# Prologue and block boundary reordered in a two-block fp32 kernel, and one mask multiply left out of the delta rule

## The reference

```
cond = silu(c); mod = cond @ w_ada + b_ada
sh1, sc1, gt1, sh2, sc2, gt2 = split(mod, 6)
h = rmsnorm(x, g_mix) * (1 + sc1) + sh1
q, k, v, qi, ki, wi, cu = split(h @ w_in)         # rope on q, k, qi, ki by positions
x = x + gt1 * (concat(attention, conformer_conv(cu)) @ w_out)
h = rmsnorm(x, g_mlp) * (1 + sc2) + sh2
x = x + gt2 * (relu(h @ w_up)**2 @ w_down)
x = rmsnorm(x, g_final)                           # end of the first block
u = rmsnorm(x, norm_mix_2); proj = u @ w_in_2     # second block
qkv = silu(causal_conv(proj[P:P+3G])); z, a, b = rest of proj
g = -exp(a_log) * softplus(a + dt_bias); gcum = cumsum(g) in chunks of 64
m = (beta*k @ k^T) * exp(gcum_i - gcum_j) where i > j else 0
attn_inner = (q @ k^T) * exp(gcum_i - gcum_j) where i >= j else 0
(I + m)^-1 applied to [beta*v, beta*k*exp(gcum)]; scan over 16 chunks
x = x + concat(pool, delta_out) @ w_out_2; MLP and norm as above
```

## Time and profile before

| what | value |
|---|---|
| median of three runs | 3015.2 us (3012.55 to 3021.21) |
| the profiled execution | 3020.86 us |
| its span | 3019.0 us |
| busy in the span: TensorE, VectorE, GpSimd, ScalarE | 93%, 58%, 41%, 23% |
| mean granted TensorE clock | 0.962 of full |
| read from HBM | 143.35 MB |

### The profile page before, as it was taken

The page is one execution under the profiler, slowest core; times in us unless marked ns, Lnnn a source line. Parts: engine busy times, 40 slices in busy tenths (PEclk is TensorE's granted clock), DMA queues, the critical chain, the costliest instruction groups (busy, mean ns, idle before and its releaser), DMA issues.

```text
span 3019.0 us, 34563 instructions
## 1 busy us (share of the span) xinstructions
PE 2808.5 (93%) x13488; PEld 2307.2 (76%) x13488; DVE 1758.3 (58%) x2240; ACT 705.0 (23%) x1154; POOL 1248.8 (41%) x815
## 2 busy tenths in 40 slices
PE   4999988899999999999997999688879999999998
PEld 4866867688778888888885767577768888888887
DVE  5257899996556665566566585255534444443335
ACT  5222233343322110000114242222214001110002
POOL 1411277453454443344347323234434443344342
PEclk8979999899999999999998999799999999999999
DMA  6200111110221111111111211000032111111111
GB/s 208 64 8 14 35 43 60 46 55 23 110 72 49 56 50 41 48 56 49 46 49 64 62 35 35 0 1 1 29 111 64 56 49 41 49 56 42 42 56 56
DMA packets 141464, 153.33 MB, mean 51 GB/s; under 512 B 6151, under 2 KB 104228, under 8 KB 141350
## 3 DMA queue, kind: packets, MB, share of 16 engines
q1 hardware_dynamic: 135360, 137.68, 14.6%
q10 hardware_dynamic: 5990, 14.09, 1.3%
HBM read 143.35 MB, written 8.39 MB: 50 GB/s over the span
## 4 chain that ended last, share of the span: by engine, by line
PE 80%; DVE 13%; ACT 3%; issue 2%; POOL 1%; DMA 0%; ACTq 0%; DVEq 0%; POOLq 0%
PE ps L1813 11%; PE ps L1814 11%; PE ps L1815 11%; PE ps L1798 11%; PE ps L1800 10%; PE ps L1799 10%; PE ps L2185 3%; DVE score L1347 3%; DVE best L1345 2%; DVE yt L1628 2%; PE ps L1878 1%; PE ps L1956 1%; PE ps L1879 1%; PE ps L1880 1%; DVE yt L1617 1%
## 5 line engine op out<-in xcount | busy, mean ns | idle before, releaser
L1798 PE MATMUL ps<-h_hi,w_hi 128*128 128x512 f32 x1472 | 592.3, 402 | 17.7 <-issue 11.7
L1800 PE MATMUL ps<-h_hi,w_lo 128*128 128x512 f32 x1472 | 578.9, 393 | 0.0
L1799 PE MATMUL ps<-h_lo,w_hi 128*128 128x512 f32 x1472 | 578.9, 393 | 0.0
L662 POOL TENSOR_TENSOR w_hi<-raw,zero 128x1024 fp32r<-128x1024 f32 x128 | 243.9, 1905 | 780.5 <-PE ps L1800 397.1
L1813 PE MATMUL ps<-w_hi,u_hi 128*128 128x512 f32 x1024 | 399.0, 390 | 0.0
L1814 PE MATMUL ps<-w_lo,u_hi 128*128 128x512 f32 x1024 | 398.8, 389 | 0.0
L1815 PE MATMUL ps<-w_hi,u_lo 128*128 128x512 f32 x1024 | 398.6, 389 | 0.0
L1521 DVE TENSOR_TENSOR act_r<-act_r 128x512 f32<-128x512 f32 x128 | 167.7, 1310 | 328.7 <-ACT act_r L1036 328.7
L1798 PEld LDWEIGHTS ps<-h_hi,w_hi 128*128 128x128 f32 x1472 | 279.7, 190 | 92.6 <-issue 28.7
L665 POOL TENSOR_TENSOR w_lo<-raw,w_hi 128x1024 fp32r<-128x1024 f32 x128 | 337.6, 2638 | 10.0
L1036 ACT ACTIVATE act_r<-ps 128x512 f32<-128x512 f32 x128 | 76.5, 598 | 1130.7 <-PE ps L1800 1130.7
(11 more groups left out here) (380 smaller groups left out, 4503.5 us busy)
## 6 DMA issues: line engine op xcount, KB each, us to landing
raw<-in_w_up_dram SPq DMA_DIRECT2D x64, 512.0 KB, 4.0
raw<-in_w_down_dram SPq DMA_DIRECT2D x64, 512.0 KB, 3.3
raw<-in_w_ada_dram SPq DMA_DIRECT2D x48, 512.0 KB, 3.7
raw<-in_w_in_dram SPq DMA_DIRECT2D x32, 512.0 KB, 3.7
raw<-in_w_out_dram SPq DMA_DIRECT2D x32, 512.0 KB, 3.3
x<-in_x_dram ACTq DMA_DIRECT2D x16, 512.0 KB, 7.6
x_mid<-x SPq DMA_DIRECT2D x8, 512.0 KB, 2.6
x<-x_mid ACTq DMA_DIRECT2D x8, 512.0 KB, 7.4
```

The costliest lines, as they stand in the source:

```text
L662: g_.tensor_tensor(w_hi[:, r, :], raw[:, r, :], zero.to_broadcast([P, 1024]), ALU.add).then_inc(sem("w_hi_done"), 1)
L1798: mm(ps[:, bank, :], wh, h_hi[:, k, cols], start=(k == 0), stop=False)
L1799: mm(ps[:, bank, :], wh, h_lo[:, k, cols], start=False, stop=False)
L1800: last = mm(ps[:, bank, :], wl, h_hi[:, k, cols], start=False, stop=(k == NK - 1))
```

## The change

Prologue: `c` is loaded straight into 128x8 by the first load of ScalarE's queue, and its sigmoid stands after the fifth; the other vectors follow. x is loaded by SP, four tiles after the first four of `w_ada` and four after the sixth. On VectorE the sums come first, without the copies and the angle ahead of them. The tap copies go to ScalarE, the cast of positions to GpSimd, the angle and sines behind `norm0`. `norm0` makes `h_f` alone and VectorE rounds it; its units go by pairs of channels, half 0 and half 1 in turn, and `tm_in(0)` waits for two units at a time. The column sums are made in two parts.

Block boundary: `times_g` goes to VectorE between partial sums 7 and 8; ScalarE writes `h_hi` alone and VectorE takes `h_lo` from PSUM; GpSimd's final scaling is left out, and x is multiplied by `rs` where it is read back (`mixed2`); `ab_half(0)` comes ahead of the turns of half 1, and TensorE goes on with 14 of 16 units.

Delta rule: the steps for g go into the loop, at columns 2, 3, 4 and 18, the first `z` before the last gate product, and the multiply of e1 by `strict` is left out (m is only read through the level masks); `qdec` comes behind `b1`.

```diff
@@ SP @@
+                if n in (4, 6):
+                    for t in range(2 * n - 8, 2 * n - 4):
+                        sp.dma_start(x[:, t, :], a["x"][0, t * P:(t + 1) * P, :]).then_inc(sem(f"x_in{t // 4}"), 16)
...
-                        sp.wait_ge(sem("x_final"), t + 1)
+                        sp.wait_ge(sem("norm_ss"), paired_ss("z", 4 * (t // 4) + 3))
@@ GpSimd @@
+            pool.wait_ge(sem("rows_in"), 16 * (len(VEC) + 3))
+            g.tensor_copy(rowsp, rowsi).then_inc(sem("rowsp_ready"), 1)
...
-            for i in range(3):
-                split2(i)
-            for t in range(4, NT):
-                times_g(t)
-            split2(3)
-            for t in range(NT):
-                pool.wait_ge(sem("norm_xn"), 2 * NT + t + 1)
-                g.tensor_scalar(x[:, t, :], x[:, t, :], rs[:, t:t + 1], None, ALU.mult).then_inc(sem("x_final"), 1)
-            for i in range(4, len(CH2)):
+            for i in range(len(CH2)):
                 split2(i)
@@ ScalarE @@
+            act.dma_start(scl[:, 1, :], a["c"].rearrange("o (k p) -> p (o k)", p=P),
+                          allow_slow_non_contiguous=True).then_inc(sem("c_in"), 16)
+            for i, (name, (r0, r1)) in enumerate(VEC.items()):
...
+                if i == 3:
+                    act.wait_ge(sem("c_in"), 16)
+                    s.activation(csil, scl[:, 1, :], ACT.Sigmoid).then_inc(sem("c_sig"), 1)
...
             for half in range(2):
-                stats(0, half, lambda e, t: e.wait_ge(sem(f"x_in{t // 4}"), 64))
+                stats(0, half, x_here)
+            for half in range(2):
                 keep(half)
+            act.wait_ge(sem("rows_tp"), 1)
+            for i in range(CONV_K):
+                o = CONV_K - 1 - i
+                s.activation(cw[:, i * NCC:(i + 1) * NCC], ps[:, 1, o * NCC:(o + 1) * NCC],
+                             ACT.Copy).then_inc(sem("cw_ready"), 1)
...
+            def norm_hi2(u):
+
+                c, half = u % NK, u // NK
+                act.wait_ge(sem("norm_turned"), 4 * NK + u + 1)
+                s.activation(h_hi[:, c, half * HALF:(half + 1) * HALF], ps[:, TURN_BANK[2][u], :], ACT.Copy,
+                             scale=vcol("norm_mix_2", c)).then_inc(sem("norm_hi"), 1)
@@ VectorE @@
+            dve.wait_ge(sem("c_sig"), 1)
+            link(v.tensor_tensor(csil, csil, scl[:, 1, :], ALU.mult))
+            ada0(0, 6)
+            inverse(0, 0)
+            ada0(6, 7)
+            inverse(0, 1)
+            dve.wait_ge(sem("rows_tp"), 2)
+            link(v.tensor_copy(vec[:, 0:NVEC], ps[:, 0, 0:NVEC]))
...
+            ada0(7, 16)
+            dve.wait_ge(sem("mod_mm"), 2)
...
+            def norm_lo2(u):
...
+                v.scalar_tensor_tensor(h_lo[:, c, cols], ps[:, TURN_BANK[2][u], :], vcol("norm_mix_2", c),
+                                       h_hi[:, c, cols].bitcast(F32), ALU.mult, ALU.subtract).then_inc(sem("norm_lo"), 1)
...
             for u in range(2 * NK):
-                c, cols = u // 2, slice((u % 2) * HALF, (u % 2 + 1) * HALF)
+                c, cols = NORM0[u]
                 dve.wait_ge(sem("norm_f"), u + 1)
+                v.tensor_copy(h_hi[:, c, cols], h_f[:, c, cols]).then_inc(sem("norm_hi"), 1)
...
-                v.tensor_tensor(x[:, t, cols], x[:, t, cols], ps[:, n % 8, :], ALU.add).then_inc(sem("x_mixed"), 1)
+                v.scalar_tensor_tensor(x[:, t, cols], x[:, t, cols], rs[:, t:t + 1], ps[:, n % 8, :], ALU.mult,
+                                       ALU.add).then_inc(sem("x_mixed"), 1)
...
+                if i == GS_AT:
+                    dve.wait_ge(sem("gs_mm"), 2)
...
+                    dve.wait_ge(sem("cm2_full"), cm2_need(len(CH2) - 1))
+                    v.tensor_tensor(prep[0]["z"], hb(tri), tb(gs["g"][:, 0, :]), ALU.mult).then_inc(prep_sem("dve", 0), 1)
@@ TensorE @@
-                        if j == 0 and t == 0:
-                            pe.wait_ge(sem("norm_lo"), 4 * kk + 4)
+                        if j == 0 and t % 4 == 0:
+                            pe.wait_ge(sem("norm_lo"), 4 * kk + 2 * (t // 4) + 2)
...
+            pe.wait_ge(sem("ab_parts"), 2)
+            ab_half(0)
             for u in range(NK, NK + 4):
                 norm_turn(2, u)
-            pe.wait_ge(sem("ab_parts"), 2)
-            ab_half(0)
             turn_again(2, NK + 4)
-            pe.wait_ge(sem("norm_hi"), 6 * NK)
+            pe.wait_ge(sem("norm_lo"), 5 * NK + 6)
...
+                if i == GS_AT:
+                    pe.wait_ge(sem("masks_ready"), 1)
+                    pe.wait_ge(sem("gs_dve"), 2)
+                    pe.wait_ge(sem("l2_sd"), 2 * GH)
```

More of the change, by code:

```diff
@@ L305, in build @@
         TURN_BANK[0] = [4 + u % 4 for u in range(2 * NK)]
+        NORM0 = [(2 * (u // 4) + u % 2, slice((u // 2 % 2) * HALF, (u // 2 % 2 + 1) * HALF)) for u in range(2 * NK)]
         TURN_BANK[2] = [c % 4 for c in range(NK)] + [(7, 1, 3, 5)[c % 4] for c in range(NK)]
@@ L752, in _ @@
                 within(level[i], 2 << i)
-            step(g.tensor_copy(strict, level[5]))
             for i in range(5, 0, -1):
@@ L1654, in _ @@
                 x0, x1 = (bank(2 * (t % SETS) + i) for i in range(2))
-                if kind == "head_z":
+                if kind == "head_z" and t:
                     if t >= SETS:
@@ L1758, in _ @@
             pe.wait_ge(sem("ident_ready"), 2)
-            pe.wait_ge(sem("rows_in"), 16 * (len(VEC) + 3))
-            nc.tensor.transpose(ps[:, 0, 0:NVEC], rowsv[0:NVEC, 0, :], ident[0:NVEC, 0:NVEC])
-            n = CONV_K * NCC
-            nc.tensor.transpose(ps[:, 1, 0:n], rowsv[0:n, 1, :], ident[0:n, 0:n])
-            n = TAPS * 12
-            nc.tensor.transpose(ps[:, 2, 0:n], rowsv[0:n, 2, :], ident[0:n, 0:n]).then_inc(sem("rows_tp"), 1)
-            pe.wait_ge(sem("rowsp_ready"), 1)
-            nc.tensor.transpose(ps[:, 3, 0:NT], rowsp, ident[0:NT, 0:NT]).then_inc(sem("rows_tp"), 1)
             def mod_cols(o, sums):
-                for part in range(2):
-                    for c in range(NK):
-                        last = mm(o[:, NK * part + c:NK * part + c + 1], sums[part][:, c * P:(c + 1) * P], ones[:, 0:1],
-                                  start=True, stop=True)
+                for c in range(len(sums) * NK):
+                    last = mm(o[:, c:c + 1], sums[c // NK][:, c % NK * P:(c % NK + 1) * P], ones[:, 0:1],
+                              start=True, stop=True)
                 last.then_inc(sem("mod_mm"), 1)
@@ L1821, in _ @@
                 norm_turn(0, u)
-            pe.wait_ge(sem("ada0_sum"), 2 * NK)
-            mod_cols(ps[:, 3, :], [mod_sum[:, part, :] for part in range(2)])
+                if u == NK - 1:
+                    pe.wait_ge(sem("rows_in"), 16 * (len(VEC) + 3))
+                    nc.tensor.transpose(ps[:, 0, 0:NVEC], rowsv[0:NVEC, 0, :], ident[0:NVEC, 0:NVEC])
+                    n = CONV_K * NCC
+                    nc.tensor.transpose(ps[:, 1, 0:n], rowsv[0:n, 1, :], ident[0:n, 0:n])
+                    n = TAPS * 12
+                    nc.tensor.transpose(ps[:, 2, 0:n], rowsv[0:n, 2, :], ident[0:n, 0:n]).then_inc(sem("rows_tp"), 1)
+                    pe.wait_ge(sem("rowsp_ready"), 1)
+                    nc.tensor.transpose(ps[:, 3, 0:NT], rowsp, ident[0:NT, 0:NT]).then_inc(sem("rows_tp"), 1)
+            for part in range(2):
+                pe.wait_ge(sem("ada0_sum"), NK * (part + 1))
+                mod_cols(ps[:, 3, NK * (2 + part):NK * (3 + part)], [mod_sum[:, part, :]])
             def tm_in(j):
```

219 lines of the change are left out of this document (99 added, 120 removed).

## The result

The changed kernel took 2975.09 us (median of 4 runs, 2969.91 to 2987.11); the kernel before took 3013.88 (4 runs, 3010.11 to 3021.21). The ratio is 0.9874, with a 95% interval from 0.9839 to 0.9909: 38.8 us less, where 34 were predicted. In microseconds that interval goes from 27 to 49, so this measurement alone doesn't tell 34 from 38.8. The profiled execution took 2974.06, its span 2972.3. Against the profiled execution of before (3020.86, span 3019.0) that is 46.7 less. So the two traces differ by 8 us more than the medians, and that has to be found first.

A forecast was written before the change was run, and what follows sets the result against it. TensorE was taken to bound the kernel (80% of the chain), with gains where it stands still. Prologue -6, block boundary -14 and delta rule's head -14 gave -34, so 2981 us from the median of 3015.2; range 2970 to 3000.

The forecast's parts named there:

- A: Prologue, up to the first projection: 6 us less, bounds 1 to 9 less.
- First sum: Prologue: with c loaded first, the first w_ada sum starts at about 5.5 us, where it was 16.10.
- Last sum: Prologue: the last w_ada sum ends at 46.3 instead of 47.36, 1.0 us less.
- Column sums: Prologue: only 16 of the 32 passes are left behind the last w_ada sum, 2.9 us less.
- Units: Prologue: TensorE waits for two normalized units, not four, taking 5 us instead of 7.2, so 2.1 less.
- What rides along: Prologue: tap copies on ScalarE, angle and sines later, cast of positions on GpSimd; they cost nothing.
- B: Block boundary, up to the second half's loop: 14 us less, bounds 8 to 18 less.
- The slow start: Loop behind the block boundary: a shorter idle stretch ahead makes its first matmuls less slow, 1.3 us less.
- C: Delta rule's head, with g's steps moved into the loop: 14 us less, bounds 9 to 15 less.
- that second term: Delta rule's head: without the strict mask's multiply and qdec ahead of it, b0 comes 1.9 us earlier.
- The warm start: Delta rule's head: a warm clock for TensorE's first two matmuls may give 0.8 us less.
- Little is held: Rival, prologue and boundary: GpSimd's port waits on VectorE are mostly missing, 40 us less in all, 2975; chance 0.13.

The follow-up runs named there:

- e1: Not a run but a value in the delta rule's code: ScalarE's output, which GpSimd multiplied by the strict mask before the change; no time of its own.
- joined: The changed kernel with later GpSimd splits, h_lo 4 to 6 between the last partial sums, two w_ada sums ahead of the second xn: 2964.33 us, ratio 0.9838.
- split_late: The changed kernel with three more waits on GpSimd, so that its splits of w_in begin later: 2973.55 us, ratio 0.9878.
- terms_back: The changed kernel with all column sums at the end, ab_half and the 16-unit wait as before, the strict mask multiplied again: 2982.92 us, ratio 0.9897.
- e2: Not a run but a value in the delta rule's code, which GpSimd makes ahead of b0; no time of its own.

## Why the prediction was right, and by what

The forecast was -34, the medians gave -38.8, inside the range; the changed kernel run once more gave -35.9 by its ratio. The sum held because its parts are independent, which was its first assumption: -37.8 from three kernels with one part each. Its terms were less good than its sum. The bounds of its parts add up to -18 and -42, not to the -39 of the text; the measured time lies inside either.

- **A, -6 against -9.1.** The first pair of traces shows -6.2, as if all were right. But the first projection stood at 60.99, 62.78, 65.00 and 65.31 in four executions of the old prologue and at 54.4 to 56.1 in four of the new, 8.5 apart in the mean. *First sum, 5.5:* measured 5.70, and this near hit is partly luck. The terms that the text names (0.8, 2.2 and two of 0.2) give 3.4. c's pieces landed 4.4 after their issue, twice the row's 2.2, and the sigmoid waited 0.76 for them, behind the other issues and a table load. *Last sum, -1.0:* this is the mis-sized term. The start of the column sums, which follow the last sum at once, moved by 2.6 in the first pair and by 3.9 between the means of four old and four new traces. In the changed kernel's trace the step that failed is ScalarE's copies ahead of the vectors' transposes. The text puts these at 33, with the vectors' copies done by 33.7. TensorE's second four turns need only the banks of the first four, so they waited for the first four copies (the first wait is the 0.66 at 28.47), where the text's 4.5 would be nine of them at 0.5 each. The vectors' copies were done at 31.9, 1.8 earlier. The nine sums behind them took 12.8, as predicted (12.6). But ahead of the last four sums VectorE waits 1.07 for a load, and in joined the same copies ended at 33.8 and the column sums still started at 44.25; so this step sets when those sums begin, and the loads set a good part of when they end. Why the old prologue was up to 4 longer in the other executions is open. *Column sums, -2.9:* -2.3 here, -1.8 when undone. *Units, -2.1:* -1.3 in the first pair (waits of 7.7 and 6.4), -1.7 to -2.2 against 8.15 and 8.64. That GpSimd holds VectorE there was right.
- **What rides along** cost nothing in the trace, as predicted; no run puts it back. The tap copies were over by 38 rather than 45: 25 of them took 1.86, so under 0.1 each, not 0.2.
- **B, -14 against -16.3.** VectorE's eighth sum ended where it was said (1566.5, in before's time 1583.5). The products ended 1.4 later than said, for the third and fourth waited 1.12 and 0.86 for ScalarE's squares of the same tile, which the working left out. They were not held. The holds were fewer: one small operation, xn (5.5 instead of 2.7) and one sum, so that xn ended at 1598.8 in before's time, between the 1596 and 1603 of the text. (The text lets every held operation end half a us after GpSimd's. In its rows that is so for the sum; the small scaling ended with GpSimd's instruction, 1600.32 and 1600.29.) The second half started at 1642.7 (predicted 1644): -14.1 for -12.7. *The slow start, -1.3,* was right in size: the loop's first pause stands 19.0 behind the loop's start in before and 17.7 in the changed kernel. The loop is 2.5 shorter because 1.7 more come from the last half-clock stretch, as in split_late, and 0.5 go to the matmuls for g that C moves into it. The text has no term for that 1.7, and three of the eight traces with part B don't show it. What the sum gave to the moved ab_half and the wait for 14 units is worth 0.5; it is the shorter unit that counts. The text had both in one line and didn't say which carried it.
- **C, -14 against -12.4.** To the first b0 it is -13.3, for -11.2 - 1.9 = -13.1, and both terms hold by themselves. From the last projection to the subtraction it is -11.4; from the subtraction's start to TensorE's first b0 5.4 us pass instead of 7.4. Of that second term the mask has 0.8 (terms_back), since m waited for the exponential and GpSimd put e2 ahead of b0. The other 1.1 are left for `qdec`, which the term counts too; no run moves `qdec` alone. *The warm start, -0.8,* failed. TensorE's start was warm (1.10 for the two matmuls that took 2.08), but that is in the -11.2 already: the subtraction began at 1874.1, with the end of VectorE's last gate product, and 2.08 would have put it at 1874.9. And the half clock came later instead: the second tile followed its first b0 after 29.0 instead of 27.6 us. Around the first two matmuls, before and after:

```profile
1916.50:1922.50 6.00, 5.52 (x18) 0.50 0.00 0
```

```profile
1872.00:1878.00 6.00, 3.15 (x18) 1.00 0.00 0
```

  And in the 26 us behind the first b0, before and after:

```profile
1926.00:1952.00 26.00, 17.67 (x94) 0.74 0.00 1
```

```profile
1879.00:1905.00 26.00, 18.43 (x90) 0.69 0.00 1
```

  In the eight traces with part C the second b0 came 28.9 to 31.1 behind the first, in the four without it 27.6 to 28.8. Later tiles gained nothing, as predicted.
- **The base.** The text put the profiled execution's excess of 5.7 over the median down to spread, and was right not to build on it: 10.8 of the traces' difference was one stretch at half clock. The excess was mostly that, less a prologue shorter than usual.
- **The rule.** The Trainium skill, "SBUF — State Buffer", section "SBUF: two separate sides", says that VectorE and GpSimd share a port pair, which whichever starts first has for its whole instruction. The text set this against a shared speed. The rows decide for the rule: 1.43 and 0.43, 2.17 and 0.17 with an end at GpSimd's own, GpSimd's 3.01 and 1.04, and h_lo out of PSUM at 2.71 and 2.72 for four with and without GpSimd beside it. *Little is held* gave nearly the right total (-40), but for the wrong reason: holds did cost time, and with the splits and h_lo moved out of each other's way (joined) it is a further -7.2 at the boundary.

## What to carry to other kernels

Before a trace becomes the base of a sum, compare its span with the median and look for stretches in which the granted clock is half while the engine is busy: here 10.8 us of one trace were of that kind, and its prologue was 2 to 4 us shorter than in others. A half-clock stretch of 3.4 us cost 1.7 or almost nothing, by whether a wait that could absorb it came behind; so a difference of that size between two traces is no term. Where a helper engine's splits have slack, tie them to a semaphore behind the main engine's SBUF operations; one wait more was worth more than the work it delayed, but only after the next two waits had been moved as well. When two edits share a line of a sum, price each: here one of them was worth 0.5, and the sum had let it count in full.

## What was not expected of the hardware

- Half clock under full load: 59 matmuls in 24 us at 0.51, in one execution only, in a stretch that ran at 1.00 in the eleven others. But another such stretch, of 17 to 20 us near 150, is in all twelve traces, with TensorE busy for 92% of it or more. In the changed kernel:

```profile
141.00:157.00 16.00, 16.00 (x36) 0.50 0.00 0
```

- The 32 column sums of one column each took 5.35, 5.89, 6.98 and 6.99 us in four executions of the same code. In parts of 16 they took 1.84 at a granted clock of 1.00 and 3.58 at 0.50.
- Waits of 0.2 to 1.5 us between TensorE's turns lengthened the start of the loop behind them by 1.3 us, at 0.85 of the clock in its first 12 us.
- ScalarE's copies of 128x4 out of PSUM: 25 in 1.86 us.
